# Written-out layers and stage borders taken token half by token half in a two-block transformer kernel

## The chip, the core and the metric

The kernel runs on one core of one Trainium2 chip. The metric is the device time of one launch in microseconds (us), as the median of several runs. All data start and end in the chip's own memory.

## What is computed

The input is `x`, 256 tokens of 1024 features in fp32. It passes through `first_block` and then `second_block`, each of two layers with weights of their own. Every layer is an FFN, a mixer and a second FFN.

```python
# first block, one layer
f = swiglu(rms_norm(h, ffn1_pre_g[l]), ffn1_w_gate[l], ffn1_w_up[l], ffn1_w_down[l])
h = h + FFN_RESIDUAL_SCALE * rms_norm(f, ffn1_post_g[l])
u = rms_norm(h, mix_pre_g[l])
(a_b, a_c, a_x, b_u, c_q, c_k, c_v, d_q, d_k, d_v, d_f, gate_logits) = _split(u @ w_in[l], IN_SPLITS)
# y_a short convolution, y_b convolution with 31 taps, y_c differential attention, y_d forgetting attention
merged = g[:, :, 0] * y_a + g[:, :, 1] * y_b + g[:, :, 2] * y_c + g[:, :, 3] * y_d
h = h + rms_norm(merged @ w_o[l], mix_post_g[l])
f = swiglu(rms_norm(h, ffn2_pre_g[l]), ffn2_w_gate[l], ffn2_w_up[l], ffn2_w_down[l])
h = h + FFN_RESIDUAL_SCALE * rms_norm(f, ffn2_post_g[l])
```

The second block has the same frame with another mixer (sliding-window attention with a bias by distance, and a gated delta rule). Its norm is a layer norm with gain and bias that is applied to the sum of the scaled residual and the stage's result, and that normed sum is the next stage's input and residual. The hidden width of every FFN is 2816.

## The kernel before

**Numbers.** Every fp32 product is made of three products of a shorter format, fp32r: high by high, high by low and low by high part (`PARTS`). So every weight and every activation needs a high part (a rounding copy) and a low part (the difference).

**Weights.** They come as a stream of units, mostly 1 MB (128 partitions by 2048 numbers), from SyncE's queue into a ring of four slots (`SLOTS`). ScalarE copies a unit's high part (`split_high`, recorded at line 1590); VectorE makes its low part (line 1913), or GpSimd for the mixers' units (line 973). A slot is given back (`slots_free`) by the first matmul of the product that follows the unit's own (`pay`, `owed`), or by `flush` where no product follows at once; only then is the next load of that slot issued.

**The order of work.** `plan_first` and `plan_second` write one layer of each block as a list of steps, and every engine walks the same list (`walk`) in a loop over the two layers (`Fori`, with semaphore values that depend on the layer's register). `Plan.close` hangs the splitting of coming units before the steps, `AHEAD` units ahead: at a step, an engine first splits the quarters listed there and then does the step's own work. Near a layer's end nothing of the next layer is split, as the list ends there.

**A stage.** An FFN has 22 gate-and-up units (`gu`, hidden block j of 128) and 11 down units (`down`, each two hidden blocks), which sum into four banks of PSUM, one for each token half t and column half n of 512. A mixer ends with four such output units (`wo`). The last of these units runs by `last_rows` (line 1164), which finishes bank after bank. ScalarE's Silu of a `gu` block is at line 1631, VectorE's split of the hidden block at line 1922.

**A border.** In the first block, ScalarE squares the stage's result (line 1638), GpSimd makes the reciprocal root (lines 927 and 929), VectorE scales, applies the gain and adds to the residual (`post`); the same three engines then take the norm of the sum (`norm`), and TensorE turns the residual by a product with a diagonal matrix of the reciprocal roots (`xt`, line 1113); the gain of the next norm is applied where the turned tiles are copied. In the second block, `post2` adds and takes the statistics (line 2209), GpSimd makes the root, VectorE scales (line 2220), and `xt` transposes (line 1115). `affine` applies gain and bias to the residual later, beside products. The first product of the next stage (line 1096 in an FFN) is column by column of weights with all 256 tokens, and starts when the turned tiles are split.

**Other work near a border.** GpSimd's queue loads the gain rows (`feature`), the parameters (`params`), and at the switch of blocks stores a table of 3 MB for the bias by distance (line 1055), which the second block's first FFN reads back in parts. Between the blocks VectorE copies the residual and makes one row of that table.

## Time and profile before

| | us |
|---|---|
| median of 3 runs | 3255.86 |
| lowest and highest | 3255.62, 3257.39 |
| the profiled execution | 3258.94 |
| its span in the profile | 3257.3 |
| TensorE busy | 3051.3 (94%) |
| VectorE busy | 1894.9 (58%) |
| ScalarE busy | 1340.1 (41%) |
| GpSimd busy | 525.3 (16%) |
| read from and written to memory | 487.31 MB, 4.19 MB: 151 GB/s over the span |
| mean granted TensorE clock | 0.965 |

### The profile page before, as it was taken

The page shows a single profiled execution, that of the slowest core. Times are in us where ns is not written, and L with a number is a line of the kernel's source. Part 1 is how long each engine was busy: PE and PEld are TensorE (multiplying, and loading weights), DVE is VectorE, ACT ScalarE, POOL GpSimd, SP SyncE. Part 2 cuts the span into 40 slices and gives each one's busy share as a digit, 9 for nine tenths or more (in the row PEclk, how much of TensorE's full clock was granted, in tenths as well). Part 3 has the DMA queues.
Part 4 walks back from the last instruction along what each step waited for, and adds up shares of the span by engine and source line. Part 5 has one row for each costly group of instructions (what it writes and reads, how often), then busy time and mean ns, then how long its engine had stood idle before and what let it go on. Part 6 is the DMA issues. An engine that isn't in the chain of part 4 may idle for free.

```text
span 3257.3 us, 59477 instructions
## 1 busy us (share of the span) xinstructions
PE 3051.3 (94%) x22178; PEld 2888.5 (89%) x22178; DVE 1894.9 (58%) x3364; ACT 1340.1 (41%) x2218; POOL 525.3 (16%) x791
## 2 busy tenths in 40 slices
PE   7999999999999999998899988989989998889998
PEld 7989998998989999897798887989989898889897
DVE  4556876555555876555455466455555546655555
ACT  4344454434334454433334543434333354443332
POOL 0000000000000000000003554550000055546100
PEclk9999999999999999999998999999999999999999
DMA  5544445454554445455663221254546522213453
GB/s 206 185 162 150 140 146 182 165 184 160 183 180 149 140 146 170 165 190 158 190 213 128 99 89 66 79 181 168 198 150 221 175 101 95 79 66 139 160 197 130
DMA packets 72445, 495.51 MB, mean 152 GB/s; under 512 B 8064, under 2 KB 8240, under 8 KB 20176
## 3 DMA queue, kind: packets, MB, share of 16 engines
q1 hardware_dynamic: 67824, 471.95, 42.2%
q0 software_dynamic: 4048, 18.59, 2.1%
q8 instruction: 184, 3.01, 0.4%
q14 instruction: 117, 0.96, 0.1%
q10 hardware_dynamic: 272, 0.99, 0.1%
HBM read 487.31 MB, written 4.19 MB: 151 GB/s over the span
## 4 chain that ended last, share of the span: by engine, by line
issue 75%; POOL 11%; PE 9%; DVE 3%; POOLq 1%; DVEq 1%; ACT 0%; DMA 0%; ACTq 0%; SPq 0%
POOL weights_low L973 9%; PE psum L1096 4%; PE psum L1153 1%; POOL small L929 1%; POOLq L928 1%; PE psum L1398 0%; PE psum L1184 0%; DVE work L2292 0%; PE psum L1404 0%; DVE work L2327 0%; PE psum L1521 0%; DVEq L2287 0%; DMA weight_ring<-stream 0%; PE psum L1509 0%; PE psum L1113 0%
## 5 line engine op out<-in xcount | busy, mean ns | idle before, releaser
L1590 ACT ACTIVATE weights_high<-weight_ring 128x2048 fp32r<-128x2048 f32 (+5 forms) x782 | 906.0, 1179 | 1109.2 <-DMA weight_ring<-stream 1101.9
L1913 DVE TENSOR_TENSOR weights_low<-weight_ring,weights_high 128x2048 fp32r<-128x2048 f32 (+4 forms) x538 | 886.9, 1655 | 785.1 <-ACT weights_high L1590 782.1
L1096 PE MATMUL psum<-normed_t_high,weights_high 128*128 128x256 f32 x2816 | 802.2, 285 | 11.6 <-DVE normed_t_low L1922 10.0
L1096 PE MATMUL psum<-normed_t_low,weights_high 128*128 128x256 f32 x2816 | 799.8, 284 | 0.0
L1096 PE MATMUL psum<-normed_t_high,weights_low 128*128 128x256 f32 x2816 | 799.6, 284 | 0.0
L1096 PEld LDWEIGHTS psum<-normed_t_high,weights_high 128*128 128x128 f32 x2816 | 542.9, 193 | 17.7 <-DVE normed_t_low L1922 12.1
L1096 PEld LDWEIGHTS psum<-normed_t_low,weights_high 128*128 128x128 f32 x2816 | 543.5, 193 | 3.2
L1096 PEld LDWEIGHTS psum<-normed_t_high,weights_low 128*128 128x128 f32 x2816 | 543.2, 193 | 0.0
L1153 PE MATMUL psum<-weights_high,work_parts 128*128 128x512 f32 x1472 | 464.3, 397 | 13.2 <-DVE work_parts L1922 13.2
L973 POOL TENSOR_TENSOR weights_low<-weight_ring,weights_high 128x256 fp32r<-128x256 f32 x560 | 413.4, 770 | 249.5 <-ACT weights_high L1590 249.4
L1184 PE MATMUL psum<-normed_t_high,weights_high 128*128 128x256 f32 x1248 | 391.7, 314 | 2.8 <-DVE normed_t_low L1922 2.1
L1184 PE MATMUL psum<-normed_t_low,weights_high 128*128 128x256 f32 x1248 | 358.4, 287 | 0.0
L1184 PE MATMUL psum<-normed_t_high,weights_low 128*128 128x256 f32 x1248 | 358.1, 287 | 0.0
L1153 PEld LDWEIGHTS psum<-weights_high,work_parts 128*128 128x128 f32 x1472 | 271.1, 189 | 71.9 <-DVE work_parts L1922 13.6
L927 POOL TENSOR_TENSOR small<-small 128x1 f32<-128x1 f32 (+3 forms) x74 | 19.6, 265 | 1872.6 <-ACT work L1638 977.4
L1153 PE MATMUL psum<-weights_low,work_parts 128*128 128x512 f32 x736 | 290.7, 395 | 0.0
L1184 PEld LDWEIGHTS psum<-normed_t_high,weights_high 128*128 128x128 f32 x1248 | 245.5, 197 | 17.3 <-issue 11.3
L1398 PE MATMUL psum<-normed_t_high,weights_high 128*128 128x256 f32 x768 | 232.9, 303 | 19.0 <-DVEq L2299 13.7
L1184 PEld LDWEIGHTS psum<-normed_t_low,weights_high 128*128 128x128 f32 x1248 | 245.7, 197 | 1.1
L1184 PEld LDWEIGHTS psum<-normed_t_high,weights_low 128*128 128x128 f32 x1248 | 244.0, 196 | 0.0
L1398 PE MATMUL psum<-normed_t_high,weights_low 128*128 128x256 f32 x768 | 219.4, 286 | 0.0
L1398 PE MATMUL psum<-normed_t_low,weights_high 128*128 128x256 f32 x768 | 219.3, 286 | 0.0
(267 smaller groups left out, 4363.8 us busy)
## 6 DMA issues: line engine op xcount, KB each, us to landing
weight_ring<-stream SPq DMA_DIRECT2D x400, 1024.0 KB, 4.9
weight_ring<-stream SPq DMA_DIRECT2D x64, 768.0 KB, 4.3
feature_rows<-feat POOLq DMA_DIRECT2D x6, 1024.0 KB, 7.4
work<-toeplitz_rows POOLq DMA_DIRECT2D x8, 512.0 KB, 6.3
feature_rows<-feat POOLq DMA_DIRECT2D x6, 512.0 KB, 4.1
toeplitz_rows<-work POOLq DMA_DIRECT2D x1, 3072.0 KB, 36.1
params<-prms POOLq DMA_DIRECT2D x5, 251.5 KB, 3.6
residual<-x SPq DMA_DIRECT2D x2, 512.0 KB, 4.3
```

The source lines that it names most:

```text
L927: pool.tensor_tensor(dst, src, EPSES[:, EPS_AT[eps], 0:n], ALU.add)
L928: pool.drain()
L929: pool.tensor_tensor(dst, dst, HALFNEG[:, 0:dst.shape[1]], ALU.pow).then_inc(signal, 1)
L973: ins = pool.tensor_tensor(LOW[at], RING[at], HIGH[at].bitcast(F32), ALU.subtract)
L1096: ins = pe.matmul(PS[:, bank, at:at + S], w[a][:, first + k, c * P:(c + 1) * P], src[b][:, k, :], start=(k, m) == (0, 0), stop=(k, m) == ( ...
L1153: ins = pe.matmul(PS[:, b, :], src[c][:, r, t * P:(t + 1) * P], w[a][:, r, n * HALF:(n + 1) * HALF], start=start and m == 0, stop=False, s ...
L1184: ins = pe.matmul(PS[:, job.bank, c * S:(c + 1) * S], w[i][:, k, c * P:(c + 1) * P], XT[j][:, k, :], start=(k, m) == (0, 0), stop=(k, m) = ...
L1398: ins = pe.matmul(PS[:, job.bank, 0:S], w[p][:, r, 0:P], XT[q][:, r, :], start=(r, m) == (0, 0), stop=(r, m) == (KB - 1, 2), skip_group_ch ...
L1590: return act.activation(dst, src, ACT.Copy, scale=scale)
L1913: dve.tensor_tensor(some(LOW, i, q, n), some(RING, i, q, n), some(HIGH, i, q, n).bitcast(F32), ALU.subtract).then_inc(low_by_vector, n)
```

## The change

- The loops over layers are written out: each engine's program holds both layers of each block, all semaphore values and addresses are constants, and splits and early loads run across the ends of layers (`unit_plan`, `earlier`). The first stage's norm and turns become a small plan of their own (`plan_start`).
- The last two down or output units of a stage are one step, `last`, which goes through the four banks and adds both units to each. In the plan both units count at this step.
- The border is a list of steps for each token half t: `post`, `norm`, `xt` in the first block, `stats`, `scaled`, `xt` in the second. Reciprocal roots are made from two half sums. In the first block the gain of the next norm is applied, with the root, to rows (`XN`), and `xt` transposes those; the gain row is loaded beside the post gain (`feat1` gets two rows a stage), so the three `g` columns leave the parameters. The diagonal product goes.
- `EARLY = 2` units of the next stage are split at the stage's end, also over layers and blocks. The steps marked `hold` have a schedule of splits of their own in `Plan.close`.
- The first two units of an FFN (`gut`) and of the first block's mixer (`cv`), and the first one of the second block's mixer (`pv`), are computed with the tokens as rows, token half by token half (`tok`, then the unit's own step): for token half 0 the first unit and half of the second, then the turns of half 1, then the rest. For an FFN the hidden blocks so made are turned back on TensorE (`hturn`).
- Moved: the residual's copy between the blocks is now part of the last `norm`; the row of the bias table is made inside the first FFN of the second block (`bias_row`), and its 3 MB store behind it; `cv`, `pv` move to their mixer's beginning; `small_split`, `factors`, `params` and `feature` move behind the early units; GpSimd's large memsets move behind the start; the merged low parts get tiles of their own (`MGL1`, `MGL2`).

The core of the diff:

```diff
-        used, high, low, short = 0, 0, 0, True
+        high = low = QUARTERS * self.early
+        used, short, first, last = 0, False, 0, QUARTERS * (self.units + EARLY)
         for n, st in enumerate(self.steps):
+            if st.hold:
+                used += st.unit is not None
+                first = used
+                if st.unit is None:
+                    continue
             if st.woven:
                 host, a = (st.src, st.a) if st.kind == "part" else (st, st.first)
                 if host.unit is None:
@@ -147,17 +155,19 @@
                 to_low = QUARTERS * (used + 1) + QUARTERS * a // host.rounds
                 to_high = to_low + 1
             else:
-                if st.unit is not None:
-                    used += 1
-                    short = any(x.kind in ("post", "post2") for x in self.steps[n + 1:n + 3])
-                to_high = QUARTERS * (used + AHEAD - short) if used or st.kind == "xt" else 0
+                if st.hold:
+                    to_high = QUARTERS * (EARLY + used)
+                else:
+                    if st.unit is not None:
+                        used += 2 if st.kind == "last" else 1
+                    short = st.kind == "last" or used <= first + 2
+                    to_high = QUARTERS * (used + AHEAD - short)
                 to_low = to_high
-            last = QUARTERS * self.units
             if min(to_high, last) > high:
                 st.high, high = quarters(high, min(to_high, last)), min(to_high, last)
...
-def plan_ffn(pl, s, after=()):
+def last_units(pl, s, kind, units, root):
+
+    pl.stream.append(units[0])
+    pl.step("last", s=s, acc=pl.named["acc", s], src=units[0], unit=units[1], what=kind, root=root)
+
+
+def early_units(pl, s, hosts, turns, small=None):
+
+    begin = len(pl.steps)
+    if len(hosts) == 2:
+        pl.steps.append(Step("tok", None, src=hosts[0], p=0, a=0, b=24))
+        pl.steps.append(Step("tok", None, src=hosts[1], p=0, a=0, b=12))
+        turns()
+        pl.steps.append(Step("tok", None, src=hosts[1], p=0, a=12, b=24))
+    else:
+        pl.steps.append(Step("tok", None, src=hosts[0], p=0, a=0, b=24))
+        turns()
+    for st in pl.steps[begin:]:
+        st.hold = True
+    for st in hosts:
+        st.hold = True
+        pl.steps.append(st)
+
+
+def plan_ffn(pl, s, turns, acc_banks, after=(), between=()):
 
     def down(j2):
         pl.step("down", ("down", s, j2), s=s, j=j2, unit=("d", s, j2))
 
-    for j in range(FB):
+    hosts = [pl.make("gut", ("gu", s, j), banks=[(6, 7) if s == 0 else (0, 1)][0][j:j + 1], s=s, j=j, rounds=24,
+                     unit=("gu", s, j), signals=[("gate_silu_ready", 1), ("hidden_rows_ready", 1)]) for j in range(2)]
+    early_units(pl, s, hosts, turns)
+    for kind, signals in between:
+        pl.step(kind, signals=signals, s=s)
+    for j in range(2, FB):
         pl.step("gu", ("gu", s, j), banks=["hi"], s=s, j=j, unit=("gu", s, j),
                 signals=[("gate_silu_ready", 1), ("hidden_ready", 1)])
-        if 2 <= j < FB - 2 and j % 2 == 0:
+        if j == 2:
+            for i in range(2):
+                pl.step("hturn", ("hturn", s, i), banks=["hi"], s=s, j=i, signals=[("hidden_ready", 1)])
+            pl.step("acc", ("acc", s), banks=acc_banks, s=s)
+        if j == 3:
+            down(0)
+        if 4 <= j < FB - 2 and j % 2 == 0:
             down(j // 2 - 1)
         for kind, signals, args in after:
             if j in args["j"]:
                 pl.step(kind, signals=signals, s=s, j=j, p=args["j"].index(j))
-    down(FP - 2)
-    down(FP - 1)
...
+    def border(s, kind, units, root):
+        last_units(pl, s, kind, units, root)
+        begin = len(pl.steps)
+        post(s, 0, root)
+        norm(s + 1, 0)
+        post(s, 1, root)
+        turns(s + 1, 0)
+        norm(s + 1, 1)
+        for st in pl.steps[begin:]:
+            st.hold = True
...
+    def border(s, kind, units):
+        last_units(pl, s, kind, units, None)
+        begin = len(pl.steps)
+        stats(s, 0)
+        scaled(s + 1, 0)
+        stats(s, 1)
+        turns(s + 1, 0)
+        scaled(s + 1, 1)
+        for st in pl.steps[begin:]:
+            st.hold = True
...
+            for l in range(LAYERS[blk]):
+                now.blk, now.l = blk, l
                 for st in PLANS[blk].steps:
                     if high is not None:
                         for i, q, n in st.high:
-                            high(i, q, n)
+                            if i < PLANS[blk].units or not final():
+                                high(i, q, n)
                     if low is not None:
                         for i, q, n in st.low:
-                            low(i, q, n)
+                            if i < PLANS[blk].units or not final():
+                                low(i, q, n)
+                    if final() and st.s == 3 and st.kind == "xt":
+                        continue
...
+            def rsqrt_of_halves(dst, halves, eps, signal, count):
+
+                for n in range(2):
+                    pool.wait_ge(squares_summed, reach("squares_summed", count + n))
+                    pool.tensor_tensor(dst, dst if n else EPSES[:, EPS_AT[eps], 0:1], halves[:, n:n + 1], ALU.add)
+                    pool.drain()
+                pool.tensor_tensor(dst, dst, HALFNEG[:, 0:1], ALU.pow).then_inc(signal, 1)
...
+            def early_product(st, s, t, a, b):
+
+                job = st.jobs[0]
+                first = (t, a) == (0, 0)
+                w = weights(st, KB, first)
+                if first:
+                    pe.wait_ge(bank_taken[job.bank], turn_at(job))
+                for n in range(a, b):
+                    k, part, low = FIRST[n]
+                    if n in (0, 8):
+                        pe.wait_ge(*lead("xt", s, t)(lambda made: (
+                            (turned_cast_ready, reach("turned_cast_ready", made.at["turned_cast_ready"] - 1 + n // 8))
+                            if now.blk == 2 else
+                            (activation_high_ready,
+                             reach("activation_high_ready", made.at["activation_high_ready"] - 1 + n // 8)))))
+                    if n in (16, 20):
+                        half = (n - 16) // 4
+                        pe.wait_ge(*lead("xt", s, t)(lambda made: (
+                            bank_taken[made.jobs[half].bank], taken_at(made.jobs[half]))))
+                    ins = pe.matmul(PS[:, job.bank, t * S:(t + 1) * S], XT[low][:, k, t * P:(t + 1) * P], w[part][:, k, :],
+                                    start=n == 0, stop=n == len(FIRST) - 1, skip_group_check=True)
+                    if n == 0:
+                        pay(ins)
+                if (t, b) == (T - 1, len(FIRST)):
+                    ins.then_inc(bank_full[job.bank], 1)
+                    owed[0] += 1
...
+            def last(st):
+
+                if st.what == "down":
+                    made = named(("gu", st.s, FB - 1))
+                    pe.wait_ge(hidden_ready, reach("hidden_ready", made.at["hidden_ready"]))
+                    src = [[h[:, a:a + 2, :] for h in (HTH, HTL)] for a in (2, 0)]
+                else:
+                    made = named(("gy", 31 if now.blk == 1 else 2 * KB - 1))
+                    pe.wait_ge(merged_ready, reach("merged_ready", made.at["merged_ready"]))
+                    merged = (MGH1, MGL1) if now.blk == 1 else (MGH2, MGL2)
+                    src = [[v[:, a:a + 2, :] for v in merged] for a in (4, 6)]
+                place = [PLANS[now.blk].place[key] for key in (st.src, st.unit)]
                 for t in range(T):
                     for n in range(2):
-                        b = jobs[2 * t + n].bank
-                        for r in range(2):
-                            for m, (a, c) in enumerate(PARTS):
-                                ins = pe.matmul(PS[:, b, :], src[c][:, r, t * P:(t + 1) * P], w[a][:, r, n * HALF:(n + 1) * HALF], start=False, stop=(r, m) == (1, 2), skip_group_check=True)
-                                if (t, n, r, m) == (0, 0, 0, 0):
-                                    pay(ins)
+                        b = st.acc.jobs[2 * t + n].bank
+                        for u, i in enumerate(place):
+                            if (t, n) == (0, 0):
+                                pe.wait_ge(low_sem(i), low_at(i))
+                            w = [v[:, i % SLOTS, :].rearrange("p (a b) -> p a b", a=2) for v in (HIGH, LOW)]
+                            for r in range(2):
+                                for m, (a, c) in enumerate(PARTS):
+                                    ins = pe.matmul(PS[:, b, :], src[u][c][:, r, t * P:(t + 1) * P], w[a][:, r, n * HALF:(n + 1) * HALF], start=False, stop=(u, r, m) == (1, 1, 2), skip_group_check=True)
+                                    if (t, n, u, r, m) == (0, 0, 0, 0, 0):
+                                        pay(ins)
                         ins.then_inc(bank_full[b], 1)
+                owed[0] += 2
+                flush()
```

## Rows read from the trace of the kernel before

**Rows 1.** The page's 40 slices: granted TensorE clock in tenths of full speed.
```profile
PEclk9999999999999999999998999999999999999999
```

**Rows 2.** Windows: us, each engine's busy time (instructions), granted clock, DMA share, GB/s.
```profile
210.95:223.53 12.58, 6.33 (x32) 6.14 (x32) 6.23 (x11) 5.21 (x11) 3.67 (x7) 0.73 0.35 125
764.43:779.10 14.67, 6.55 (x33) 6.55 (x33) 10.94 (x13) 10.16 (x14) 3.89 (x7) 0.65 0.34 112
1519.30:1534.50 15.20, 4.47 (x19) 3.39 (x19) 11.74 (x12) 6.43 (x9) 6.38 (x7) 0.66 0.51 128
1740.31:1751.20 10.89, 3.93 (x16) 3.14 (x16) 7.25 (x13) 1.94 (x5) 1.48 (x4) 0.70 0.27 97
2189.15:2199.40 10.25, 4.04 (x17) 3.04 (x17) 6.76 (x12) 2.05 (x5) 1.51 (x4) 0.63 0.28 103
2390.45:2403.30 12.85, 3.67 (x16) 3.28 (x16) 9.01 (x10) 2.00 (x5) 0.89 (x3) 0.61 0.26 87
```

**Rows 3.** Windows behind that last border and in dense work.
```profile
2403.34:2406.80 3.46, 3.46 (x16) 3.46 (x17) 2.89 (x6) 3.12 (x5) 0.00 (x0) 0.50 0.00 0
2407.30:2413.00 5.70, 5.70 (x48) 5.68 (x48) 5.04 (x4) 2.30 (x3) 0.00 (x0) 1.00 0.11 20
```

**Rows 4.** Timeline, TensorE at the first border: start, busy us, instruction [idle before <-releaser].
```profile
217.07 6.33 PE L1113 MATMUL psum<-work,residual 128*128 128x128 f32 x32 [6.12 <-DVE work L1907]
```

**Rows 5.** Timeline, the other engines at the first border.
```profile
205.31 1.92 ACT L1590 ACTIVATE weights_high<-weight_ring 128x2048 fp32r<-128x2048 f32 x1 [4.05 <-DMA weight_ring<-stream]
207.32 2.29 DVE L1913 TENSOR_TENSOR weights_low<-weight_ring,weights_high 128x2048 fp32r<-128x2048 f32 x1 [2.73 <-ACT weights_high L1590]
209.90 0.56 POOL L929 TENSOR_TENSOR small<-small 128x1 f32<-128x1 f32 x1 [0.23 <-issue]
212.23 1.04 POOL L927 TENSOR_TENSOR small<-small 128x1 f32<-128x1 f32 x1 [1.77 <-ACT work L1638]
```

**Rows 6.** Costliest groups by form: count, busy us, mean ns, idle before.
```profile
L1590 ACT ACTIVATE work<-psum 128x512 f32<-128x512 f32 x42 | 24.7, 587 | 23.8 <-PE psum L1184 11.4 <-PE psum L1466 6.3 <-PE psum L1201 6.0
L2209 DVE SCALAR_TENSOR_TENSOR work<-psum,residual 128x512 f32<-128x512 f32 x24 | 16.4, 682 | 10.9 <-PE psum L1164 10.4 <-issue 0.5
L1590 ACT ACTIVATE work<-psum,small 128x128 f32<-128x128 f32 x48 | 14.1, 365 | 30.8 <-DVE small L2321 30.8
```

**Rows 7.** Timeline ahead of the first border, one engine each.
```profile
199.59 0.63 PE L1153 MATMUL psum<-weights_high,work_parts 128*128 128x512 f32 x2
200.89 0.36 ACT L1631 ACTIVATE work<-psum 128x256 f32<-128x256 f32 x1
204.17 0.42 DVE L1922 TENSOR_TENSOR work_parts<-work,work_parts 128x256 fp32r<-128x256 f32 x1
```

**Rows 8.** Timeline at the end of the last FFN.
```profile
3232.68 0.63 PE L1153 MATMUL psum<-weights_high,work_parts 128*128 128x512 f32 x2
3234.26 0.43 DVE L1922 TENSOR_TENSOR work_parts<-work,work_parts 128x256 fp32r<-128x256 f32 x1
```

**Rows 9.** Timeline at the end of each block's first mixer.
```profile
553.23 0.43 DVE L1922 TENSOR_TENSOR work_parts<-work,work_parts 128x256 fp32r<-128x256 f32 x1
557.72 0.63 PE L1164 MATMUL psum<-weights_high,work_parts 128*128 128x512 f32 x2
...
2177.73 0.42 DVE L1922 TENSOR_TENSOR work_parts<-work,work_parts 128x256 fp32r<-128x256 f32 x1
```

**Rows 10.** Timeline at the start of the kernel.
```profile
11.87 1.89 ACT L1590 ACTIVATE weights_high<-weight_ring 128x2048 fp32r<-128x2048 f32 x1
22.51 0.36 PE L1096 MATMUL psum<-normed_t_high,weights_high 128*128 128x256 f32 x1 [0.36 <-DVE normed_t_low L1941]
```

**Rows 11.** Timeline and transfers (KB each, median us to landing) from 1529 to 1570.
```profile
1570.43 1.22 PE L1153 MATMUL psum<-weights_high,work_parts 128*128 128x512 f32 x2 [13.21 <-DVE work_parts L1922]
...
toeplitz_rows<-work POOLq DMA_DIRECT2D x1, 3072.0 KB, 36.1
weight_ring<-stream SPq DMA_DIRECT2D x3, 1024.0 KB, 18.3
```

565 lines of the change are left out of this document (318 added, 247 removed).

## Prediction

> **What bounds the kernel now.** I read the page's slices first, then TensorE's idle time at the stage borders (windows), then the other engines there (timeline), then lines for durations. The granted clock stands at 9 or more in nearly every slice [rows 1]: dense stretches run at the full rate, 48 matmuls of 256 columns in 5.7 us, 0.12 us each [rows 3]. What is lost lies at the borders between stages, and I count a border from the last matmul of one stage's final row product to the first matmul of the next stage's product. The six windows shown stand for eleven [rows 2]: 12.6 us inside a layer of the first block (four such, 11.8 to 12.6), 14.7 at its layer end, 15.2 at the switch of blocks, 10.9 (two, into the mixer), 10.3 (two, into the FFN) and 12.9 in the second block; about 134 us in all. In each TensorE first idles, 6.12 us at the first border [rows 4], while ScalarE, GpSimd and VectorE take the norm in turns [rows 5]; then the turns themselves run with the clock at 0.61 to 0.73 [rows 2]. In the second block it also comes back slowly: 16 matmuls in 3.46 us at clock 0.50, 0.216 us each [rows 3], so about 2 us more are lost behind the window (22 such matmuls at 0.216 instead of 0.12); behind the first block's borders nothing is.
>
> **Durations used.** Copying a weight unit high takes ScalarE 1.92 us, its low part VectorE 2.29 [rows 5]. A 512-column copy takes ScalarE 0.59, a 512-column PSUM operation VectorE 0.68, a drain between two about 0.1, a 512-column scaling out of SBUF some 0.45 (estimate, two thirds of that), a 128-column ScalarE operation 0.37 [rows 6] and about 0.31 apart when four follow each other (estimate). A rsqrt on GpSimd is 0.19, 0.56 and gaps, 1.15 us from request to answer [rows 5]. A turn of 128 columns costs 0.11 at full clock (estimate: 32 in 6.33 us at a granted clock that had fallen, 0.198 each [rows 4], bounded by half of that).
>
> **The new wait at an FFN's end.** Before, the last two down units are two steps. The first of them covers the wait for the last hidden block: it starts at 199.59, ScalarE's Silu of that block starts at 200.89, behind the copy of the unit after next, and the hidden parts are ready at 204.60 [rows 7]. Now both units are one product that begins only when the last hidden block is there, while the copies ahead of the Silu and of the multiplication keep their place. So TensorE waits 5.1 us (204.60 + 0.1 - 199.59). At a layer's end this was short before, since nothing of the next layer was split there: at the very end the block is ready at 3234.69, 2.0 us behind its product at 3232.68 [rows 8]. Written out, the layer ends split the next layer's units and pay 5.1 too; only the last FFN pays 2.1. At a mixer's end one output unit of 5.6 us still covers the wait: the merged block is ready at 553.65, its product ended at 546.7 (557.72 is the start of the last unit, with two of 5.6 us ahead of it), so 1.4 us stay; in the second block 2178.15 against 2177.8, 0.4 us [rows 9].
>
> **The border behind it, counted from the merged product's start.** It runs 48 matmuls of 512 columns, 11.2 us; token half 0 is summed at 5.6. But the slot of the second early unit is freed only by this product's first matmul. Before, the same load took from 199.59 to 205.31 [rows 5, 7], so the high copy ends at 7.6, the low one at 10.0, and both stand ahead of the norm work on their queues. First block: two gains to 11.3, residual halves at 12.1 and 12.9, squares to 13.6, rsqrt 14.75, normed halves 15.4 and 16.1, four turns behind each, high copies, first early product at 16.8. Its high part lasts to 18.7; the low part waits for VectorE, which has token half 1's gains and sums in front, until 19.8 and 20.4; then half a unit, the turns of half 1 (ready 21.6), and no wait more. TensorE does 7.5 us of work between 11.2 and 24.7: idle 6.0, and the 16 turns cost 1.8. Second block: statistics 10.0 to 13.1, rsqrt, scaled 14.7, turns to 15.8; cast only behind token half 1's statistics (15.1 to 18.2), first product 18.7, and later waits are short: idle 7.0, turns 1.8. Into the mixer there is a single early unit, so nothing covers the affine copies of half 1: idle 8.6. An FFN behind a border also turns two hidden blocks back, 0.6 us. Where the clock falls it is mostly hidden in these waits in the first block; I take 0.5 to 1.5 us a border in the second.
>
> GpSimd's first add took 1.04 us, not about 0.2, while VectorE added the residual [rows 5]. The Trainium skill, SBUF — State Buffer, section "SBUF: two separate sides", says that VectorE with two SBUF inputs locks GpSimd out of a shared port for the whole instruction. The trace agrees; by this rule a rsqrt could come 0.85 us later at each of the first block's six borders, 5 us in all; by the order above VectorE is idle or busy elsewhere then, and the sum takes none.
>
> **Sum**, gains first:
> - First block, mixer to FFN, twice: 12.6 against 1.4 + 6.0 + 1.8 + 0.6 = 9.8: 5.6.
> - Its layer end: 14.7 against 5.1 + 6.0 + 1.8 + 0.6 = 13.5: 1.2. About 2 us of the 14.7 are the loop's turning back, as the windows inside a layer are that much shorter.
> - The switch: 15.2 + 2 slow against 13.5: 3.7 (the copy of the residual, the bias row and its wait are off the chain).
> - Second block, mixer to FFN, twice: 10.3 + 2 against 0.4 + 7.0 + 1.8 + 0.6 + 1.5 = 11.3: 2.0.
> - The start: the first product now begins at 22.51 [rows 10]. The halves of x need no diagonal, GpSimd's large memsets move behind; the first unit's high copy begins at 11.87 [rows 10], so 1.9 + 2.3 later its low part is there, about 16; the second unit comes 4 us behind. I take 5 (2 to 7).
> - Immediate wait values for register ones: nothing dense waits on them; 1 (0 to 6).
> - FFN to mixer: first block 12.2 against 12.9, twice: -1.4. Second block 10.9 + 2.3 against 5.1 + 8.6 + 1.8 + 0.5 = 16.0, twice: -5.6.
> - Second block's layer end: 12.9 + 2 against 15.2: -0.3.
> - The end: -2.1, and +1.2 as token half 0's statistics are done early: -0.9.
> - The Toeplitz store of 3 MB, issued ahead of the second block's first units, takes 36.1 us; the three weight loads behind it take 18.3 (median) instead of 5, and TensorE idles 13.21 us [rows 11]. It now goes out behind the second early unit, a unit later in TensorE's work, and the border's slots are partly used up: 2 more (-4 to 13).
>
> 5.6 + 1.2 + 3.7 + 2.0 + 5 + 1 - 1.4 - 5.6 - 0.3 - 0.9 - 2 = 8.3 less. Other moved work (parameter and feature loads, the double feature row of 1 MB, the convolution taps, small split, factors, POOL's low parts, which fall to other units in equal number) lies beside 5.7 us products and is put at nothing; uncovered, a feature load would cost some 5 us once. Profiled: 3258.94 (span 3257.3 and 1.6 around it) - 8.3 = 3250.6; the median of the runs shown is 3.1 lower: 3247.6, rounded to 3247. The main unknowns: 1 us in the chain behind the merged product counts ten times, 10 us either way.
>
> **Rivals.**
> - *Slower: the clock stays down through the border.* TensorE now works in pieces of 1 to 3 us with waits between. If the clock is at 0.5 from the wait ahead of the merged product until the early units are done, the 7.5 us of turns and early products take 13.4, of which some 2.5 fit into waits: 3.4 more at each of ten borders, less the 5 already counted, 29 more: 3276. It decides against the change once more than 2 us a border are lost. For it: the clock fell in every border window [rows 2]. Against: work now follows the fall early. Chance 0.17.
> - *The store starves the early FFN.* Nothing of the ring moves while the store runs, and TensorE has three units in hand instead of four: 5.7 + 5 more, 3256. For it: 13.21 us of idle with four in hand [rows 11]. Chance 0.15. The Trainium skill, DMA: Bandwidth & Descriptors, section "Queues, rings and completion order", says an engine drains a whole packet, some 9 to 17 descriptors, of one ring before it turns to another; by that rule a load waits long whenever the store is ahead, which the 18.3 us agree with.
> - *The 5.1 us wait isn't there*, because the last hidden block comes before the copies: 3247 - 7 x 5.1 = 3211. Against: the order of the steps leaves the copies ahead of the Silu [rows 7]. Chance 0.08.
> - The forecast: 0.60, with a range of its own of 3237 to 3259.
>
> **How the numbers follow.** A measurement of this kernel can tell about 0.2%, 6.5 us: faster is below 3249.3, slower above 3262.4. Of the forecast's 0.60 I put 0.36 below, 0.21 within and 0.03 above; the starved store 0.03, 0.10 and 0.02; the clock 0.17 above, less 0.04 within; the missing wait 0.08 below; faster 0.47, same 0.35, slower 0.18. The range 3228 to 3268 leaves out most of the missing wait and the worst of the clock.
>
> **What would show it.** In the profile after: an idle of about 5.1 us ahead of the merged product at seven FFN ends and about 2 at the eighth; ScalarE's squares starting 7.6 us behind its start, not at 2.8; border idle of 6 and 7 to 8.6 us behind it; clocks of 0.6 to 0.8 there; the first product at 16 to 18. The prediction is wrong if the wait ahead of the merged product is short, if the second early unit is there early, or if the store's stall grows.

## The result and the profile after

The changed kernel takes 3267.93 us as the median of 20 runs, the kernel before 3256.99 beside it; the ratio is 1.0033, with a 95% interval of 1.0023 to 1.0042. So it is 0.3% slower, where 3247 and "faster" were forecast; the time lies at the very top of the stated range. The profiled execution took 3270.15, with a span of 3268.3, 11.0 more than before. The runs also spread wider: 3256.5 to 3282.9, against 3253.9 to 3263.0. (The forecast started from 3255.86, a median of 3 runs of the kernel before; the median of 20 is 1.1 higher.)

The page of the changed kernel, its span, its busy times and the granted clock by slice (the line that answers to [rows 1]):

```profile
span 3268.3 us, 54720 instructions
PE 3047.7 (93%) x22114; PEld 2876.6 (88%) x22114; DVE 1916.4 (59%) x3377; ACT 1350.0 (41%) x2289; POOL 539.3 (17%) x822
PEclk9999999999999999999998999999999999999999
```

TensorE is busy 3.6 us less than before (3051.3), in a span 11.0 longer, so the loss is waiting. TensorE's waits in the changed kernel (line that waited, what it waited for, us in total, times, longest):

```profile
PE psum L1348 <- DVE work_parts L2116: 39.8, 10, 5.3
PE psum L1239 <- DVE work L2099: 29.4, 6, 12.5
PE psum L1263 <- DVE normed_t_high L2133: 17.4, 17, 2.7
PE psum L1585 <- DVEq L2516: 14.3, 4, 4.5
PE psum L1239 <- DVE work L2445: 10.6, 5, 3.1
```

Line 1348 is the merged product, 1239 the turns, 1263 the early products and 1585 a product of the second block's gate units. The first row is the new wait ahead of the merged product: seven of the ten are 4.8 to 5.3 us long.

Where the 11 us come from is read by the starts of the same products in both traces. The columns are the change that was forecast and the one measured, in us.

| stretch | forecast | measured |
|---|---|---|
| start to the sixth gate-and-up unit | -5 | -2.0 |
| first block, both layers, end of FFN 1 to FFN 2 | -4.2 | -4.2 |
| first block's layer end | -1.2 | +1.1 |
| switch of blocks, with the bias table's store | -1.7 | -5.7 |
| second block, first layer, end of FFN 1 to FFN 2 | +1.8 | +13.5 |
| second block, second layer, the same | +1.8 | +2.1 |
| second block's layer end | +0.3 | +2.6 |
| the end | +0.9 | +2.8 |
| registers; dense stretches | -1 | +0.8 |
| sum | -8.3 | +11.0 |

More than half of the gap of 19.3 is one row. The two layers of the second block run the same program, and one of them is 11.4 us worse than the other. Matched matmul by matmul, 8.8 of these come within 31 us, around the first score of that mixer; the rest comes later in small steps. Timeline of the changed kernel there, GpSimd, VectorE and TensorE (start, busy us, instruction, in brackets the idle time before it and what ended it):

```profile
1767.51 25.09 POOL L1095 TENSOR_TENSOR weights_low<-weight_ring,weights_high 128x256 fp32r<-128x256 f32 x32 [23.93 <-ACT weights_high L1767]
1768.02 1.05 DVE L2420 TENSOR_TENSOR residual<-work,feature_rows 128x512 f32<-128x512 f32 x1
...
1783.27 0.42 DVE L2317 CUSTOM_DVE_ANT_0 work<-psum,work 128x256 f32<-128x256 f32 x1
1783.77 8.85 DVE L2321 TENSOR_SCALAR small<-small 128x2 f32<-128x2 f32 x1
1792.54 0.28 DVE L2315 CUSTOM_DVE_ANT_0 work<-psum,work 128x128 f32<-128x128 f32 x1
...
1793.69 0.90 PE L1496 MATMUL psum<-constants,work 128*128 128x128 f32 x3 [8.02 <-ACT work L1889]
```

An operation on 128 by 2 numbers takes VectorE 8.85 us; most of its other instances take about 0.3. It ends at 1792.62, and GpSimd's run of 32 low-part pieces, which has no gap in it, ends at 1792.60. Other operations of VectorE were not held like this: the one at 1768.02, with both inputs in SBUF, took 1.05 us beside the same run instead of 0.69. In the second layer the run begins at 2635.73, and the first score falls in the same place of it, 16.24 us behind its start (16.26 in the first layer). Yet here the same operation passes, and a later one of the same run is held:

```profile
2651.96 0.67 DVE L2321 TENSOR_SCALAR small<-small 128x2 f32<-128x2 f32 x1
2653.72 0.30 DVE L2321 TENSOR_SCALAR small<-small 128x2 f32<-128x2 f32 x1
2657.52 3.39 DVE L2321 TENSOR_SCALAR small<-small 128x2 f32<-128x2 f32 x1
```

That last one ends at 2660.91, and the run at 2660.88. Two kernels below keep this run of 32 pieces (the last unit's own work first, and the slot paid at once), which makes six such mixers in three traces. At 16.25 us behind the run's start the operation took 8.85 us twice and 0.67 or 0.68 four times. In those four, the one at 21.8 to 22.1 us was held instead, for 3.15 to 3.40. What decides between the two isn't shown.

Before, GpSimd's run at this place had 16 pieces and 11.1 us. It had twice as many after, because the second block's mixer now begins with `pv` at a border: its next four units all fall to GpSimd and are there together, and GpSimd needs 6.3 us for one.

The first border follows the forecast's chain closely. The changed kernel's windows of the wait, of the merged product and of what follows (us, then busy time and instructions of PE, PEld, DVE, ACT, POOL, then granted clock, DMA share, GB/s), which answer to [rows 2], and its timeline on ScalarE and VectorE:

```profile
197.86:203.18 5.32, 0.00 (x2) 0.00 (x1) 3.34 (x4) 1.55 (x2) 0.00 (x0) 0.98 0.00 0
203.18:216.09 12.91, 12.91 (x48) 10.01 (x48) 4.98 (x5) 3.79 (x7) 2.53 (x3) 0.88 0.23 82
216.09:227.12 11.03, 8.04 (x54) 7.65 (x55) 6.84 (x11) 4.97 (x13) 3.94 (x10) 0.85 0.51 192
```

```profile
197.23 1.91 ACT L1767 ACTIVATE weights_high<-weight_ring 128x2048 fp32r<-128x2048 f32 x1 [2.96 <-DMA weight_ring<-stream]
199.04 0.37 ACT L1817 ACTIVATE work<-psum 128x256 f32<-128x256 f32 x1
208.88 1.91 ACT L1767 ACTIVATE weights_high<-weight_ring 128x2048 fp32r<-128x2048 f32 x1 [9.47 <-DMA weight_ring<-stream]
210.70 0.58 ACT L1825 ACTIVATE work<-psum 128x512 f32<-128x512 f32 x1
...
210.89 2.29 DVE L2107 TENSOR_TENSOR weights_low<-weight_ring,weights_high 128x2048 fp32r<-128x2048 f32 x1 [7.77 <-ACT weights_high L1767]
217.97 1.42 DVE L2099 SCALAR_TENSOR_TENSOR work<-residual,small,feature_rows 128x512 f32<-128x512 f32 x2 [1.86 <-POOL small L1050]
```

The Silu starts at 199.04, behind a copy of 1.91 us. Counted from the merged product's start at 203.18, the second early unit's high copy ends at 7.6 (forecast 7.6), its low part at 10.0 (10.0), the squares start at 7.5 (7.6), the normed halves end at 16.2 (16.1), and the first early product starts at 17.2 (16.8). What was not in the sum is the merged product's own length: 12.75 us here instead of 11.2, as the clock falls in the wait ahead of it.

### The profile page after: what moved, and what is told of

Same layout as the page of the kernel before. It is cut to its first block, busy times and chain, and to the rows that moved or that the text cites. A ratio compares the mean times of both kernels' runs of the same rounds, so it can differ in the third digit from the quotient of the medians.

```text
span 3268.3 us, 54720 instructions
## 1 busy us (share of the span) xinstructions
PE 3047.7 (93%) x22114; PEld 2876.6 (88%) x22114; DVE 1916.4 (59%) x3377; ACT 1350.0 (41%) x2289; POOL 539.3 (17%) x822
## 4 chain that ended last, share of the span: by engine, by line
issue 65%; PE 19%; DVE 7%; POOL 3%; DMA 2%; ACT 2%; DVEq 1%; POOLq 1%; ACTq 0%
PE psum L1367 4%; PE psum L1217 3%; POOL weights_low L1095 2%; PE psum L1263 2%; PE psum L1585 2%; PE psum L1323 1%; PE psum L1591 1%; DMA toeplitz_rows<-work 1%; DVE work L2509 1%; PE psum L1689 1%; DMA weight_ring<-stream 1%; PE psum L1701 1%; PE psum L1481 1%; POOLq L1049 1%; PE psum L1699 1%
## 5 line engine op out<-in xcount | busy, mean ns | idle before, releaser
L1217 PE MATMUL psum<-normed_t_high,weights_high 128*128 128x256 f32 x2560 | 725.1, 283 | 0.0
L1217 PE MATMUL psum<-normed_t_high,weights_low 128*128 128x256 f32 x2560 | 723.9, 283 | 0.0
L1217 PE MATMUL psum<-normed_t_low,weights_high 128*128 128x256 f32 x2560 | 723.9, 283 | 0.0
L1217 PEld LDWEIGHTS psum<-normed_t_high,weights_high 128*128 128x128 f32 x2560 | 490.5, 192 | 4.0 <-issue 0.6
L1217 PEld LDWEIGHTS psum<-normed_t_low,weights_high 128*128 128x128 f32 x2560 | 490.6, 192 | 3.4
L1217 PEld LDWEIGHTS psum<-normed_t_high,weights_low 128*128 128x128 f32 x2560 | 490.7, 192 | 0.0
L1323 PE MATMUL psum<-weights_high,work_parts 128*128 128x512 f32 x1280 | 403.7, 396 | 10.3 <-DVE weights_low L2107 10.3
L1367 PE MATMUL psum<-normed_t_high,weights_high 128*128 128x256 f32 x1248 | 389.5, 312 | 2.8 <-POOL weights_low L1095 2.3
L1367 PE MATMUL psum<-normed_t_low,weights_high 128*128 128x256 f32 x1248 | 357.5, 286 | 0.0
L1367 PE MATMUL psum<-normed_t_high,weights_low 128*128 128x256 f32 x1248 | 356.8, 286 | 0.0
L1323 PEld LDWEIGHTS psum<-weights_high,work_parts 128*128 128x128 f32 x1280 | 235.5, 189 | 62.0 <-DVE weights_low L2107 10.5
L1367 PEld LDWEIGHTS psum<-normed_t_high,weights_high 128*128 128x128 f32 x1248 | 244.3, 196 | 16.3 <-issue 11.9
L1323 PE MATMUL psum<-weights_low,work_parts 128*128 128x512 f32 x640 | 253.5, 396 | 0.0
L1585 PE MATMUL psum<-normed_t_high,weights_high 128*128 128x256 f32 x768 | 232.5, 303 | 20.2 <-DVEq L2516 14.3
L1367 PEld LDWEIGHTS psum<-normed_t_low,weights_high 128*128 128x128 f32 x1248 | 244.5, 196 | 1.1
L1367 PEld LDWEIGHTS psum<-normed_t_high,weights_low 128*128 128x128 f32 x1248 | 243.1, 195 | 0.0
L1585 PE MATMUL psum<-normed_t_low,weights_high 128*128 128x256 f32 x768 | 218.8, 285 | 0.0
L1585 PE MATMUL psum<-normed_t_high,weights_low 128*128 128x256 f32 x768 | 218.7, 285 | 0.0
L1048 POOL TENSOR_TENSOR small<-small 128x1 f32<-128x1 f32 x52 | 21.8, 419 | 1000.9 <-ACT work L1825 965.4
```

Of the source, the lines that this page charges most:

```text
L1217: ins = pe.matmul(PS[:, bank, at:at + S], w[a][:, first + k, c * P:(c + 1) * P], src[b][:, k, :], start=(k, m) == (0, 0), stop=(k, m) == ( ...
L1323: ins = pe.matmul(PS[:, b, :], src[c][:, r, t * P:(t + 1) * P], w[a][:, r, n * HALF:(n + 1) * HALF], start=start and m == 0, stop=False, s ...
L1367: ins = pe.matmul(PS[:, job.bank, c * S:(c + 1) * S], w[i][:, k, c * P:(c + 1) * P], XT[j][:, k, :], start=(k, m) == (0, 0), stop=(k, m) = ...
L1585: ins = pe.matmul(PS[:, job.bank, 0:S], w[p][:, r, 0:P], XT[q][:, r, :], start=(r, m) == (0, 0), stop=(r, m) == (KB - 1, 2), skip_group_ch ...
```

## Experiments

All but the last are edits of the changed kernel. Each has several timed runs, and its ratio is to the kernel before. The 95% intervals are in brackets.

### The last unit's own work first

```diff
                 for st in PLANS[blk].steps:
+                    own_first = st.kind == "gu" and st.j == FB - 1 and st.kind in kinds
+                    if own_first:
+                        kinds[st.kind](st)
...
+                    if own_first:
+                        continue
```

> At the last gate-and-up unit of an FFN, ScalarE takes its Silu and VectorE its product and split of the hidden block ahead of the copies of the next unit. Theory (the copies ahead of the Silu make the wait): the idle time ahead of the merged product falls from 4.8 to 5.5 us at seven FFN ends to the 2.0 us of the last one, where no copy stands ahead: 7 x 3.0 = 21 us less than the changed kernel's 3268, so 3247. Rival (the clock that falls in this wait is what costs): the merged product, 12.8 to 14.0 us long now, goes back to 11.3 and the borders behind it gain that too, up to 2 us at each of eight: 3233 to 3240. Rival (the wait only moves, since the second early unit's load or the first one's copies then end last): less than 5 us are gained, 3263 or more.

Measured: 3247.83, ratio 0.9977 (0.9965 to 0.9989). Timeline of this kernel at the first border (here line 1822 is the Silu and 1353 the merged product):

```profile
197.25 0.38 ACT L1822 ACTIVATE work<-psum 128x256 f32<-128x256 f32 x1 [3.44 <-PE psum L1222]
197.53 1.90 ACT L1772 ACTIVATE weights_high<-weight_ring 128x2048 fp32r<-128x2048 f32 x1
...
199.03 0.73 PE L1353 MATMUL psum<-weights_high,work_parts 128*128 128x512 f32 x2 [1.81 <-DVE work_parts L2121]
```

The wait is 2.0 us at all eight FFN ends, and the gain of 20.1 over the changed kernel agrees with the 7 x 3.0 of the theory. At five of the eight ends the merged product is back at 11.3 us, and yet nothing more is gained: the borders behind it start from the second early unit's copy, so the half-speed stretch was hidden there. This shows that the order of the copies makes the wait. That the clock in this wait cost little while the load hid it is read from the sum; the runs, from 3242.1 to 3260.3 with GpSimd's long runs still in them, are too wide to tell a few us.

### Gaps in GpSimd's low parts

```diff
                         if part % 2:
                             ins.then_inc(low_by_pool, 1)
+                            pool.drain()
```

> GpSimd drains after every second piece of a low part, so that it no longer runs 32 pieces (25 us) without a gap. Theory (VectorE's small operation at line 2321, 8.85 us instead of 0.26 in the second block's first mixer, is held up by GpSimd's unbroken run): no VectorE operation is longer than 3 us, TensorE's 8.0 us of idle ahead of line 1496 go, with the clock that fell behind it 9 us, and 1 to 2 in the second layer: 3258. Rival (it waited for something else, such as its code or the bias rows): the 8.85 us stay, 3268. Rival (GpSimd is the bound of that stretch and the drains make it slower): its low parts take over 6.3 us a unit, waits for them grow: 3270 or more.

Measured: 3272.01, ratio 1.0043 (1.0026 to 1.0059), so the number missed. The trace shows both halves of it: no VectorE operation is held up any more, neither at the score nor elsewhere, and TensorE's 8 us of idle are gone. But in the gate units GpSimd now ends last. TensorE's waits for GpSimd's low parts in this kernel, and in the changed kernel below it:

```profile
PE psum L1586 <- POOL weights_low L1095: 15.6, 4, 5.5
```

```profile
L1585 PE MATMUL psum<-normed_t_high,weights_high 128*128 128x256 f32 x768 | 232.5, 303 | 20.2 <-DVEq L2516 14.3 <-POOL weights_low L1095 4.9 <-DVE weights_low L2107 0.8
```

That is 15.6 us of waiting against 4.9. The theory and the second rival were both right in their mechanisms, and both prices were set too low, as the next experiment shows.

### Gaps in the input units only

```diff
                             ins.then_inc(low_by_pool, 1)
+                            if unit_plan(i)[0].stream[unit_plan(i)[1]][0] == "w":
+                                pool.drain()
```

> The changed kernel with GpSimd's drains only in the low parts of the second block's input units, not in its gate units, where the drains in every unit made TensorE wait 5.4 us twice for a low part. Theory (the unbroken run holds VectorE up, worth 9 us where it does; the drains' own price was in the gate units): neither long wait: 3272 - 2 x (5.4 + 1.5 for the clock) = 3258, with no VectorE operation at the score step over 2 us, and runs that lie within 5 us of each other in place of 26. Rival (the held-up operation cost nothing that the next wait doesn't take): 3268 with the same spread.

Measured: 3252.63, ratio 0.9989 (0.9980 to 0.9998), with ten runs from 3249.5 to 3257.2, where the changed kernel's spread over 26 us. No operation of the score step is over 2 us in either layer. This one edit takes 15.3 us off the median of the changed kernel. By the starts of the same products, the two stretches with the second block's mixers (fifth and sixth row of the table) are 15.0 and 4.2 us shorter than in the changed kernel's trace. It is 19.4 us faster than the kernel with drains everywhere, so that is what the drains in the gate units cost by the medians (of 10 and 4 runs), where the expectation took 2 x 6.9.

Kernels that still have the runs of 32 pieces fit that: the profiled execution of the kernel with the slot paid at once (below) has 3.40 and 3.38 us at its two scores and took 3241.3, the lowest of its ten, while the others reach 3263.7. So a typical execution should have the long hold in one layer or both. That is inferred from the spread and from three traces (8.85 and 3.39, 3.15 and 8.85, 3.40 and 3.38), as not every execution left one. The clock is a part of it: in the changed kernel's runs the mean granted clock goes from 0.972 in the fastest to 0.966 in the slowest, and in this kernel's it stays at 0.972 to 0.974. The runs don't separate what the waiting costs from what the lower clock behind it costs.

### One low part moved to VectorE

```diff
-            self.by.append("pool" if key[0] in self.by_pool and not after_ffn else "vector")
+            begin = next((n for n, k in enumerate(self.stream) if k[0] == "w"), 0)
+            self.by.append("pool" if key[0] in self.by_pool and not after_ffn and i != begin + 5 else "vector")
```

> The changed kernel without any drain; in the second block's mixer the low part of the third of the four units that GpSimd makes in one unbroken run (32 pieces, 25 us) is made by VectorE instead. Theory (the length of the unbroken run is what holds VectorE up at the score step, and the drains helped by breaking it): the run is cut to 16 pieces and 8, no operation at the score step is longer than 3 us in either layer, TensorE's 8 us of idle there are gone, and the time is that with drains in the input units, 3253, plus up to 2 x 2.3 us for the low part on VectorE: 3253 to 3258, within 8 us of each other. Rival (the drains helped in another way, for instance by shifting GpSimd's work in time): the 8.9 us stay in one layer or both: 3268, with runs 26 us apart.

Measured: 3266.42, ratio 1.0029 (1.0019 to 1.0039). No operation at the score step is over 0.9 us in either layer, and the runs lie within 10.4 us. The first layer's stretch is 6.4 us shorter than in the changed kernel, but the second layer's is 5.6 longer. Timeline of this kernel, the moved low part in the first layer and then the second layer:

```profile
1777.71 2.74 DVE L2108 TENSOR_TENSOR weights_low<-weight_ring,weights_high 128x2048 fp32r<-128x2048 f32 x1 [7.69 <-ACT weights_high L1768]
...
2629.45 12.40 POOL L1096 TENSOR_TENSOR weights_low<-weight_ring,weights_high 128x256 fp32r<-128x256 f32 x16 [23.18 <-ACT weights_high L1768]
...
2638.99 5.01 DVE L2108 TENSOR_TENSOR weights_low<-weight_ring,weights_high 128x2048 fp32r<-128x2048 f32 x1 [6.82 <-ACT weights_high L1768]
...
2650.90 0.90 PE L1497 MATMUL psum<-constants,work 128*128 128x128 f32 x3 [5.06 <-ACT work L1890]
```

In the second layer the low part that was moved takes 5.01 us instead of 2.29: it waits for the end of GpSimd's run, now 16 pieces, at 2641.85, and then needs its 2.2 us. TensorE then idles 5.06 us at the score. In the first layer the same low part took 2.74 beside such a run, so being caught is again not certain. The runs of 32 had held an operation at the score in six mixers of six, and the shorter ones none in two, as in the theory. The time missed the theory's 3253 to 3258, and only a part of that is found: both layers are slower than with the drains in the input units, by 8.6 and 9.8 us, of which 2.5 and 3.0 are there right behind the first score and the rest comes in small steps later.

### The slot of the last unit paid at once

```diff
                 cols_product(job.bank, S, w, 1, XT, KB).then_inc(bank_full[job.bank], 1)
                 owed[0] += 1
+                if st.j == FB - 1:
+                    flush()
```

> The ring slot of an FFN's last gate-and-up unit is given back as soon as its own product is done, and not by the first matmul of the merged product, 5 us later. Theory (the load of the second early unit ends last in the chain behind the merged product's start): its high copy ends at 2.6 us behind that start instead of 7.6, ScalarE's squares start at 5.7 instead of 7.5, VectorE's statistics at 5.7 instead of 10: 1.8 us at four ends of the first block and about 4 at three of the second, 19 us less: 3249. Rival (the merged product's own sums, late by the clock that fell, take its place): squares at 7.1, statistics at 7.1, 4 x 0.4 + 3 x 3 = 10 less: 3258. Rival (another wait behind it takes its place at once): no change.

Measured: 3252.85, ratio 0.9989 (0.9974 to 1.0004), 15.1 less than the changed kernel, between the theory's 19 and the first rival's 10; the runs spread over 22 us, so the median doesn't decide between them. ScalarE at the first border in this kernel, whose merged product starts at 203.99 (1769 copies a unit, 1827 squares):

```profile
203.67 1.91 ACT L1769 ACTIVATE weights_high<-weight_ring 128x2048 fp32r<-128x2048 f32 x1 [3.46 <-DMA weight_ring<-stream]
208.77 0.60 ACT L1827 ACTIVATE work<-psum 128x512 f32<-128x512 f32 x1 [3.19 <-PE psum L1350]
...
211.57 0.60 ACT L1827 ACTIVATE work<-psum 128x512 f32<-128x512 f32 x1 [2.11 <-PE psum L1350]
```

The copy ends 1.6 us behind the start instead of 7.6, and the squares now wait for the product itself. The second one starts at 7.6, not at 5.7, since the clock has fallen: here, with the load out of the way, the half-speed stretch does cost. By this timeline both accounts hold, one behind the other.

### The three together

The last unit's own work first, the drains in all of GpSimd's units, and the slot paid at once.

> The three edits together. Theory: 21 (wait ahead of the merged product 2.0), 10 (no VectorE operation held up), and for the slot less than alone, since the merged product starts 3 us sooner: high copy done at 6.7 behind its start, low part at 9.0, 4 x 0.8 + 3 x 1 = 6: 3231. Rival (they hide one another or the clock takes its place): 3245 or more.

Measured: 3231.86, ratio 0.9924 (0.9907 to 0.9940); the four runs lie within 3.6 us. The theory's 3231 came out. The drains' price in the gate units is still in it (15.7 us of TensorE's waits for GpSimd's low parts there, the longest 5.4).

### The wait covered

The drains only in input units, and the merged product's order changed for token half 0:

```diff
+                order = [(0, n, 0) for n in range(2)] + [(0, n, 1) for n in range(2)]
+                order += [(1, n, u) for n in range(2) for u in range(2)]
+                pe.wait_ge(*cover)
+                for t, n, u in order:
...
+                    if (t, n) == (0, 0):
+                        if u:
+                            pe.wait_ge(*whole)
```

> The three edits together, the drains only in input units, and in the merged product the first unit's part of token half 0 (12 matmuls, 2.8 us) runs ahead of the wait for the last hidden or merged block; both banks of that half are still summed after 24 matmuls. From the 3232 of the three edits: 14 less for the drains in gate units, 3218. Theory (behind the merged product's start the second early unit's copy ends last, 7 us behind the last gate-and-up unit whatever the merged product does): the wait of 1.97 us goes, but the border keeps its length, 0.5 us each at most: 3214. Rival (the 2.0 us are gained in full at eight ends and 1.2 at four): 3198. Rival (the wait only moves into the middle of the product): 3218.

Measured: 3209.04, ratio 0.9852 (0.9837 to 0.9867), 1.5% faster than the kernel before and 1.8% faster than the changed one. The wait ahead of the merged product is 0.4 us at all eight FFN ends, and none opens inside it. How much that gained is not isolated, as two things changed at once. Of the 22.8 us gained over the three together, the drains in the gate units make 19.4 by the medians above, which leaves 3.4. The traces say the same: from one to the other the two stretches with the second block's mixers, where those drains were, are 19.4 us shorter, and all others together are 1.2 longer. So covering the wait brought a few us at most, though 8 x 1.6 us of it went. That fits the theory's 4 at most and not the rival's 20. The time still came out below the theory's 3214, because the drains had been taken at 14. ScalarE at its first border (the merged product starts at 198.07):

```profile
197.85 0.39 ACT L1833 ACTIVATE work<-psum 128x256 f32<-128x256 f32 x1 [3.28 <-PE psum L1224]
198.13 1.91 ACT L1783 ACTIVATE weights_high<-weight_ring 128x2048 fp32r<-128x2048 f32 x1
202.77 1.92 ACT L1783 ACTIVATE weights_high<-weight_ring 128x2048 fp32r<-128x2048 f32 x1 [2.72 <-DMA weight_ring<-stream]
204.59 0.58 ACT L1841 ACTIVATE work<-psum 128x512 f32<-128x512 f32 x1
```

The second early unit's load and copy end last again, 6.6 us behind the start, against 5.6 for the sums. What is left at the borders hangs on that load.

### The loops alone

The kernel before with `for l in range(L)` in place of its `Fori` loops, and nothing else of the change.

> The kernel before with its loops over layers written out, and nothing else. Theory (as the prediction took it: the loop's turning back costs 2 us at a layer end, and register values 1 in all): two layer ends are 2 us shorter each, 3257 - 5 = 3252. Rival (nothing waits on either, and the longer program costs nothing): 3257. Rival (the longer program costs something in the dense stretches, which are 0.1 us longer each in the changed kernel): 3258 or more.

Measured: 3259.54, ratio 1.0009 (1.0000 to 1.0018). The first block's layer end got 1.1 us longer, the second block's 2.1 shorter, the start 0.5 shorter, the switch 2.8 longer, the first block's second layer 2.3 longer and the second block's two 1.3 and 1.7 shorter; the dense stretches stayed the same to 0.01 us. Writing out the loops gains nothing in all. The prediction took the 2 us more at the first block's layer end for the loop's turning back, and they don't go with the loop; whether the 2.1 of the second block's are the loop's, beside changes of the same size elsewhere, isn't shown. The 1 us credited to constants isn't seen either, and the 0.1 us of the changed kernel's dense stretches comes from something else in it.

## Why the prediction was wrong, point by point

- **The wait at FFN ends** was right in cause and size: 5.1 forecast, 4.8 to 5.3 measured at seven ends and 2.0 at the last. The experiment that removes its cause gained 20.1, where 21 were expected.
- **The chain behind the merged product** was right to 0.4 us at the first border, and the two layers of the first block came out at -4.2, as summed.
- **The step that failed** is the one in which moved work "lies beside 5.7 us products and is put at nothing", with "POOL's low parts, which fall to other units in equal number". The grouping was not equal: four units in one run instead of two. A small operation of VectorE's score step was held by that run, for 8.85 us in one layer and 3.39 in the other, and TensorE idled 8.0 us behind the first of them. The rows to see it were there, as GpSimd's first add at a border took 1.04 us beside a VectorE operation [rows 5]; the prediction cited the port rule for VectorE shutting GpSimd out and never asked for the other direction. It was visible before, too. The timeline of the kernel before, in a gate unit:

```profile
2142.59 6.29 DVE L1922 TENSOR_TENSOR work_parts<-work,work_parts 128x256 fp32r<-128x256 f32 x1
...
2142.99 5.61 POOL L973 TENSOR_TENSOR weights_low<-weight_ring,weights_high 128x256 fp32r<-128x256 f32 x8
```

  An operation of 0.43 us takes 6.29 beside eight GpSimd pieces that end at 2148.60. A group's mean hid it. In the changed kernel the same place holds VectorE's low part, 7.41 and 7.36 us instead of 2.29, which costs TensorE under 1 us. The term that was put at nothing is worth 15.3 us in the median (the drains in input units), 15.0 and 4.2 in the two layers of the profiled execution. Without it the time is 3252.6, and the forecast's sign holds, though by 0.1% only. The Trainium skill, SBUF — State Buffer, section "SBUF: two separate sides", says that of a GpSimd operation and a VectorE operation that needs the port they share (one with two inputs in SBUF, for example), whichever starts first has it for the whole instruction and blocks the other. The traces agree that one blocks the other, but not on how long or on who: the operation at 1783.77 was held until the last of 12 further pieces had ended, 0.69 us apart, and the one at 2142.59 began 0.40 us ahead of the first of the eight pieces that it waited for (GpSimd was issuing a load just then).
- **The residual gap** is made of small terms. The start gained 2.0, not 5. The early products do begin 5.3 us sooner, at 17.2 (forecast 16 to 18), but 22 of them run at 0.21 us instead of 0.12; before, this slow time fell on turns. The changed kernel's windows of its first 36 early products with eight turns, and of the 65 matmuls behind them:

```profile
17.21:24.52 7.31, 7.31 (x44) 7.31 (x45) 3.34 (x3) 0.10 (x1) 1.08 (x2) 1.00 0.78 305
24.52:31.95 7.43, 7.43 (x65) 7.43 (x64) 4.47 (x5) 6.25 (x6) 0.00 (x0) 1.00 0.21 66
```

  44 instructions there take the time of 65.
- **The clock** had a rival of its own (3276), and its place was guessed wrongly. It falls in the wait ahead of the merged product, which then takes 12.75 to 14.0 us at seven of the FFN ends and 12.85 at the last. In the first block that is hidden by the second early unit's copy. At the very end nothing hides it: +1.6 of the +1.9 missing there; in the kernel with the slot paid at once this product took 11.3 and the end was 1.5 us shorter. Into the second block's mixers the sum took 2.3 us for the lower clock before and 0.5 after. Both are too small: TensorE works for far longer at clock 0.50, where half of the time is lost. Windows of the kernel before behind the two borders, and of the changed kernel:

```profile
1761.80:1771.90 10.10, 10.10 (x49) 10.10 (x49) 0.56 (x5) 3.46 (x8) 3.06 (x5) 0.50 0.17 69
2615.10:2625.30 10.20, 10.20 (x49) 10.20 (x49) 0.76 (x7) 3.76 (x8) 2.96 (x5) 0.50 0.14 60
```

```profile
1756.10:1766.20 10.10, 10.10 (x49) 10.10 (x49) 1.03 (x10) 4.10 (x8) 0.00 (x0) 0.50 0.13 52
2626.50:2633.20 6.70, 6.70 (x33) 6.70 (x33) 0.56 (x5) 2.90 (x6) 0.00 (x0) 0.50 0.03 10
```

  Both terms are short by several us, the two errors nearly cancel, and the second layer as a whole is off by only 0.3.
- **The layer ends**, 2.3 us worse than forecast each. In the first block's, the load of the second early unit took 7.4 us instead of the usual 4.8, and that load is bare in this design. The kernel with one low part moved to VectorE has the same program there; its load took 4.7, and its stretch is 2.9 us shorter. Why the load is slow in some executions is open, and so is the second block's 2.3.
- **The bias table's store** was put at 2 worse and was 2.9 better: the idle time behind it is 10.3 us where it was 13.21 [rows 11]. The row of it in the changed kernel's waits is this; the rest of the switch was 2.8 less, against 3.7.

```profile
PE psum L1323 <- DVE weights_low L2107: 10.3, 1, 10.3
```

- **The rivals.** "The 5.1 us wait isn't there" and "the store starves the early FFN" fell. So did the clock's rival as a whole, since the mean granted clock rose from 0.965 to 0.970, though it named a real loss in a wrong place: the merged products are 1.4 to 2.7 us longer for it. None of them was the mechanism that decided.
- **Small slips in the sums.** The layer end of the second block, 15.2, has 0.7 us for the clock in it that are not named. The clock's rival puts 7.5 us of work at half rate at 13.4, where it would be 15.0. And 3247.6 was rounded down. None of them changes a conclusion.

## What to carry to other kernels

Look at the longest instance of each small operation, not at group means: one that ends just when another engine's run ends may be held by it, and removing the run or putting gaps in it tells. If a reordering bunches a neighbour's background work, its length between gaps matters as much as its sum; a drain every microsecond or two cost 19 us here where that engine was the bound, and nothing that was seen elsewhere. When a step waits for the last block of the stage before, let that block's own operations run ahead of any prefetch on their queues, and give back a buffer when its last reader is done, not when the next product begins.

## What the hardware showed that was not expected

- An unbroken run of GpSimd operations that read and write SBUF can hold a VectorE operation with its operands there until the run ends: 8.85 us and 3.39 (runs of 32 pieces), 5.01 instead of 2.29 (16 pieces), and in the kernel before 6.29 instead of 0.43 (8 pieces). It holds few of them. Beside the same runs most took 0 to 0.6 us more (1.05 instead of 0.69 at 1768.02), and an operation at the same place of the run within 0.02 us was held in two mixers and passed in four. A VectorE operation with one of its two operands in PSUM took no longer than elsewhere during the same run (0.42 us at 1783.27). With drains after every second piece in all units no such hold is left in the trace.
- Runs of the three kernels with the run of 32 pieces spread over 18 to 26 us; with the drains in the input units, over 8. That the hold makes this spread is inferred.
- The first 22 matmuls of the kernel before and the first 30 of the changed one take 0.21 us each, whatever they are, though the granted clock reads 1.00 there after the change.
- The load of a 1 MB unit took 4.7 to 5.1 us at most borders. At the first block's layer end it took 7.4, 6.8 and 7.4 us in three traces (the changed kernel and the two with drains and no other edit), 4.7 to 5.0 in four others and 5.9 in the last; at the switch of blocks 4.9 in the changed kernel and 6.0 to 7.4 in four other traces.
